# Head preparation and softmax rows in the projection's run of a two-block transformer kernel

## The chip, the cores and the metric

The kernel runs on one core of a Trainium2 chip. The metric is the device time of one execution in microseconds. A core has a matrix engine (TensorE, PE in the profile), VectorE (DVE), ScalarE (ACT) and GpSimd (POOL), and a queue engine, SyncE (SP), which here only issues DMAs. ScalarE issues a few DMAs too. Every engine runs its own list of instructions in order; semaphores order them against each other.

## What is computed

The reference is a pair of transformer blocks over 512 tokens of width 1024. The part that matters is the attention of the first block. One projection gives the inputs of three mixers (batch left out, 64 wide heads):

```
h = rms_norm(x, norm_mix);  proj = h @ w_in
a_q, a_kv, a_g, b_qkv, c_qkv = split(proj)
# a: 4 query heads on one key head, three branches: compressed, selected, window
#    q and k normed per head; compressed keys/values = gelu((kv + pe) @ w1) @ w2
# b: dilated heads, 3 groups of 2, q and k normed per head
#    s = q.k * scale - slope * distance;  p = softmax(s);  out = p @ v
# c: stick breaking, 6 heads:
#    z = q.k * scale;  a = exp(log_sigmoid(z) + sum_after(log_sigmoid(-z)))
cat = concat([o_a, o_b, o_c]);  x = x + cat @ w_out
```

Then come the squared-ReLU layer, and a second block with a recurrence, a convolution, two cross attentions and two gated feed-forward layers. None of that is touched.

## The kernel before

Matrices in full precision are split into a rounded high half and a rest, both of a rounded float32 type, and multiplied in three passes (hi·hi, hi·lo, lo·hi). That is `Linear`: for every output tile of 128 rows it does 24 matmuls of 512 columns. Weights come from SP in chunks of 512 KB, four slots deep; ScalarE makes the high half of a chunk two chunks ahead (`split_hi`), GpSimd the rest (`split_lo`). Small products that are not split run in plain float32.

`Projection` hangs on the `Linear` that makes the 24 projection tiles, in the order of `TILES`: stick tiles first, then queries, keys and values of the other mixers, three value tiles last. Functions are called once a tile on each engine: `in_tensor` after a tile's matmuls, `in_scalar` after ScalarE's split of the step, `in_vector` (which evicts the tile from its PSUM bank, t mod 4), and `in_pool`. From tile 6 on, three tiles carry one of the six stick heads: after part 0's tile TensorE does the values of the head before and this head's scores (`z`), ScalarE takes absolute values and exponentials, in part 1 ScalarE takes logarithms and VectorE the softplus, and after part 2's tile TensorE sums logarithms with a triangular matrix (`accumulate`), which waits for VectorE's remainders (`softplus_rest`, signal `softplus_lo`). Head 5 has tiles 21, 22 and 23, so its sums come after the last tile, and its values after that.

`run` gives one block of the program: all engines meet at its end. Three blocks follow each other: the projection, then `prepare_mixers`, then `softmax_mixers`. `prepare_mixers` loads the compression weights `cw` (2 MB), a table of picks, and the distance tables `dist`, all from SP. ScalarE squares ten tiles; TensorE sums the squares by head (L1119), turns four value tiles (L1110), does the compression (L1127), and spreads the inverse roots over a tile's rows (`L1140`, plain float32, four PSUM banks); VectorE takes the reciprocal (L1195) and multiplies (L1198). `softmax_mixers` takes four blocks of 128 queries, with 18 rows of scores each. It is staged one block ahead: scores of block qb + 1 stand among the transposes and values of block qb, and two packed tiles of the output projection (`partial`) stand before the first transpose. For a row TensorE writes scores (L1287), VectorE adds the distances and takes the minimum (`biased`, L1358), ScalarE takes exponentials (L1430), VectorE makes the weights of the 18 rows together (`weigh`), GpSimd and VectorE scale, and TensorE transposes (L1303).

## Time and profile before

| | |
|---|---|
| median of 3 runs | 2438.26 us (2438.21 to 2439.14) |
| the profiled execution's own time | 2442.83 us |
| its span, first to last instruction | 2441.1 us |
| TensorE busy | 2346.0 us (96%) |
| VectorE, ScalarE, GpSimd busy | 1124.9, 945.9, 1083.5 us |
| mean granted TensorE clock | 0.986 of full |
| end of the last projection tile | 203.6 us |
| first instruction of the preparation, of the softmax rows | 211.6, 240.7 us |

Busy shares are means over very different stages: what a change in one stage is worth is read from what TensorE waits for there, and for how long. The granted clock is 1.00 (2.4 GHz) or 0.50 (1.2 GHz); a value between them is a stretch that has both.

### The profile page before, as it was taken

What the parts mean: (1) busy time and instruction counts of PE and PEld (TensorE: products, weight loads), DVE (VectorE), ACT (ScalarE), POOL (GpSimd) and SP (SyncE); (2) the same over time, 40 slices, a digit from 0 to 9 for tenths busy, and PEclk for the clock granted to TensorE, in tenths of its full rate; (3) what the DMA queues carried; (4) which work ended last, traced back from release to release, by engine and by line L of the source; (5) the groups of instructions that cost most, each with busy time, mean ns of one, the idle gap of its engine ahead of it and who ended that gap; (6) DMA issues with size and microseconds to landing.
All of it is one profiled execution on the core that took longest, in us unless ns stands there. A gap on an engine that the chain in (4) does not pass through costs nothing.

```text
span 2441.1 us, 35228 instructions
## 1 busy us (share of the span) xinstructions
PE 2346.0 (96%) x13656; PEld 1866.7 (76%) x13656; DVE 1124.9 (46%) x1866; ACT 945.9 (39%) x1586; POOL 1083.5 (44%) x936
## 2 busy tenths in 40 slices
PE   7999999999989998989999999999999999999998
PEld 5776567888866777859878888888668777888887
DVE  5234544203125698535233660552697432651462
ACT  3565563212227563444333231233234534232222
POOL 4341455444541343337625445346235525445444
PEclk9999899999999999999999999999999999999999
DMA  3222002222421210024312223232113222223222
GB/s 130 70 69 92 18 27 95 95 95 95 154 84 35 69 61 10 3 84 133 104 44 87 95 95 112 78 104 97 60 60 122 78 69 77 89 93 114 78 101 69
DMA packets 57372, 198.10 MB, mean 81 GB/s; under 512 B 6544, under 2 KB 10768, under 8 KB 56592
## 3 DMA queue, kind: packets, MB, share of 16 engines
q1 hardware_dynamic: 54288, 191.70, 23.4%
q10 hardware_dynamic: 2944, 4.48, 0.5%
q8 instruction: 95, 1.56, 0.3%
q14 instruction: 45, 0.37, 0.1%
HBM read 194.05 MB, written 2.10 MB: 80 GB/s over the span
## 4 chain that ended last, share of the span: by engine, by line
PE 48%; DVE 6%; ACT 1%; issue 0%; POOL 0%; DVEq 0%; ACTq 0%
PE ps L370 11%; PE ps L372 11%; PE ps L371 11%; DVE ps L3005 4%; PE ps L445 3%; PE ps L447 3%; PE ps L446 3%; PE ps L2848 1%; PE ps L2871 1%; PE ps L3018 1%; DVE ps L3167 0%; PE ps L2608 0%; PE ps L2858 0%; PE ps L3062 0%; PE ps L2612 0%; DVE ps L2983 0%
## 5 line engine op out<-in xcount | busy, mean ns | idle before, releaser
L469 POOL TENSOR_TENSOR w_lo<-raw,w_hi 128x512 fp32r<-128x512 f32 x342 | 448.2, 1310 | 936.4 <-ACT w_hi L461 936.2
L370 PE MATMUL ps<-ahead_hi,w_hi 128*128 128x512 f32 x1216 | 481.3, 396 | 1.9 <-issue 1.9
L372 PE MATMUL ps<-ahead_hi,w_lo 128*128 128x512 f32 x1216 | 473.6, 389 | 0.0
L371 PE MATMUL ps<-ahead_lo,w_hi 128*128 128x512 f32 x1216 | 473.4, 389 | 0.0
L470 POOL TENSOR_TENSOR w_lo<-raw,w_hi 128x512 fp32r<-128x512 f32 x342 | 452.0, 1322 | 0.0
L461 ACT ACTIVATE w_hi<-raw 128x1024 fp32r<-128x1024 f32 x342 | 353.0, 1049 | 171.9 <-PE ps L447 91.0
L738 DVE TENSOR_TENSOR x_stream<-x_stream,ps 128x512 f32<-128x512 f32 x79 | 54.3, 688 | 469.9 <-PE ps L372 279.4
L370 PEld LDWEIGHTS ps<-ahead_hi,w_hi 128*128 128x128 f32 x1216 | 228.4, 188 | 52.7 <-issue 6.4
L371 PEld LDWEIGHTS ps<-ahead_lo,w_hi 128*128 128x128 f32 x1216 | 228.5, 188 | 50.7 <-issue 4.1
L372 PEld LDWEIGHTS ps<-ahead_hi,w_lo 128*128 128x128 f32 x1216 | 228.4, 188 | 47.8
L3139 ACT ACTIVATE ffn_s<-ps 128x512 f32<-128x512 f32 x44 | 26.3, 598 | 322.3 <-DVE ps L3167 322.3
L445 PE MATMUL ps<-ffn_a_hi,w_hi 128*128 128x512 f32 x342 | 133.6, 391 | 3.0 <-DVE ffn_a_lo L3172 2.9
L3005 DVE SCALAR_TENSOR_TENSOR ps<-conv_u,vecs,ps 128x512 f32<-128x512 f32 x192 | 127.1, 749 | 14.5 <-PE ps L3018 14.5
L446 PE MATMUL ps<-ffn_a_lo,w_hi 128*128 128x512 f32 x342 | 133.2, 389 | 0.0
L447 PE MATMUL ps<-ffn_a_hi,w_lo 128*128 128x512 f32 x342 | 133.2, 389 | 0.0
L775 POOL TENSOR_TENSOR squares<-squares,sqr 128x512 f32<-128x512 f32 x55 | 73.2, 1331 | 111.0 <-ACT sqr L764 65.6
L3150 DVE TENSOR_TENSOR ffn_u<-ps,root 128x512 f32<-128x512 f32 x88 | 60.6, 688 | 133.2 <-PE ps L372 133.1
L3167 DVE SCALAR_TENSOR_TENSOR ps<-ffn_u,vecs,ps 128x512 f32<-128x512 f32 x176 | 119.8, 749 | 0.0
L370 PE MATMUL ps<-hidden_hi,w_hi 128*128 128x512 f32 x256 | 99.7, 389 | 0.0
L371 PE MATMUL ps<-hidden_lo,w_hi 128*128 128x512 f32 x256 | 99.6, 389 | 0.0
L372 PE MATMUL ps<-hidden_hi,w_lo 128*128 128x512 f32 x256 | 99.6, 389 | 0.0
L370 PE MATMUL ps<-h_hi,w_hi 128*128 128x512 f32 x192 | 78.8, 410 | 16.3 <-DVE w_lo L251 13.8
(454 smaller groups left out, 4486.3 us busy)
## 6 DMA issues: line engine op xcount, KB each, us to landing
raw<-in_wall SPq DMA_DIRECT2D x346, 512.0 KB, 3.3
x_stream<-in_x SPq DMA_DIRECT2D x8, 256.0 KB, 7.6
cw<-in_cmp_w SPq DMA_DIRECT2D x1, 2048.0 KB, 7.8
out_y<-x_stream SPq DMA_DIRECT2D x16, 128.0 KB, 1.9
lora_a<-in_lora_a ACTq DMA_DIRECT2D x1, 1280.0 KB, 10.4
dist<-in_consts SPq DMA_DIRECT2D x1, 1088.0 KB, 10.9
lora_b<-in_lora_b ACTq DMA_DIRECT2D x1, 1024.0 KB, 5.1
mem<-in_mem SPq DMA_DIRECT2D x1, 1024.0 KB, 5.9
```

Source lines behind the costliest of these rows:

```text
L370: pe.matmul(out, hi, src.hi[:, t, 0:width], start=first, stop=False)
L371: pe.matmul(out, hi, src.lo[:, t, 0:width], start=False, stop=False)
L372: return pe.matmul(out, lo, src.hi[:, t, 0:width], start=False, stop=last)
L445: pe.matmul(out, hi, src.hi[:, q, 0:width], start=(q == 0), stop=False)
L446: pe.matmul(out, hi, src.lo[:, q, 0:width], start=False, stop=False)
L447: mm = pe.matmul(out, lo, src.hi[:, q, 0:width], start=False, stop=(q == kt - 1))
L461: e.activation(self.w.hi[:, s, :], self.raw[:, s, :], ACT.Copy).then_inc(hi_r.sem, 1)
L469: e.tensor_tensor(self.w.lo[:, s, 0:512], self.raw[:, s, 0:512], as_float(self.w.hi[:, s, 0:512]), ALU.subtract)
L470: e.tensor_tensor(self.w.lo[:, s, 512:1024], self.raw[:, s, 512:1024], as_float(self.w.hi[:, s, 512:1024]), ALU.subtract).then_inc(lo_r.se ...
L775: e.tensor_tensor(k.squares[:, :], k.squares[:, :], sqt[:, m % 2, :], ALU.add).then_inc(ac.sem, 1)
L3005: v.scalar_tensor_tensor(bank, self.u[:, m, t:t + T], self.tap(m, t), bank, ALU.mult, ALU.add).then_inc(self.added.sem, 1)
L3167: e.scalar_tensor_tensor(bank, ub[:, m % 4, t:t + T], col, bank, ALU.mult, ALU.add).then_inc(cv.sem, 1)
```

## The change

The two blocks after the projection become stages of the projection's run, `Heads` and `Softmax`; no border is left between the three. What moves:

- Squares go from ScalarE to VectorE, one tile behind the eviction, into tiles and value places that are free by then. The compression weights come in four pieces, with three small tensors, by seven DMAs that ScalarE issues in its step 7. The picks (10 x 128 columns) become 20 columns, which ScalarE expands.
- After tile 20 TensorE does the compression; after tile 21 the head sums and the small products; ScalarE takes GELU in step 20 and the roots in step 21; VectorE the reciprocal in step 21.
- The inverse roots are kept as a rounded value and a rest, in rows 32 apart, so that spreads run in the rounded type. Three spreads stand after tile 22, ahead of the last stick head's accumulation; the other seven stand among the matmuls of tile 23. VectorE multiplies after the last head's remainders.
- The distance tables lie where the projection's inputs were. SP loads them after tile 23's matmuls.
- The first 18 rows of scores have places of their own: 16 need no eviction, rows 16 and 17 wait for eight biased rows. After them come the last head's values and the four turns of value tiles, then two scores of the next block and the partial products.

The core of the diff:

```diff
+    def load(self, act):                      # Heads
+        self.done(act.dma_start(self.pos[:, :], a["cmp_pe"]), "cmp_small", 16)
+        self.done(act.dma_start(self.w2[:, :], a["cmp_w2"]), "cmp_small", 16)
+        self.done(act.dma_start(self.fan_raw[:, :], a["consts"][:, c:c + 2 * HEAD_TILES]), "cmp_small", 16)
+        for j, n, t in self.w1:               # four pieces
+            self.done(act.dma_start(t[:, :, :], a["cmp_w1"][:, j:j + n, :]), "cmp_loaded", 16)
...
         # Projection.in_tensor
-        if h >= 0 and part == 2:
+        if h >= 0 and part == 2 and h < self.H - 1:
             for u in range(4 * h, 4 * h + 4):
                 self.accumulate(pe, u)
+        if t == N_PROJ - 4:
+            self.heads.compress(pe)
+        elif t == N_PROJ - 3:
+            self.heads.summed(pe)
+        elif t == N_PROJ - 2:
+            self.heads.begin_spreads(pe)
+            for u in range(4 * h, 4 * h + 4):
+                self.accumulate(pe, u)
+
+    def amid(self, pe, t, q):
+        if t == N_PROJ - 1 and q:
+            self.heads.spread(pe, q + 2)
...
         # in_scalar
+        if t == self.FIRST + 1:
+            self.heads.load(act)
...
+        if t == N_PROJ - 4:
+            self.heads.gelu(act)
+        elif t == N_PROJ - 3:
+            self.heads.roots(act)
+        elif t == N_PROJ - 2:
+            self.heads.rounded(act)
...
         # in_vector, ahead of the eviction
+        if t >= 1:
+            self.heads.square(v, t - 1)
+        if t == N_PROJ - 2:
+            self.softplus(v, h)
+            self.heads.rests(v)
         v.wait_ge(self.used.sem, self.used(t + 1))
...
+        if t == 12:
+            self.heads.raws(v)
+        elif t == N_PROJ - 3:
+            self.heads.inverses(v)
+        elif t == N_PROJ - 2:
+            for n in range(HEAD_TILES):
+                self.heads.normed(v, n)
...
     def sync(self, sp):
-        pass
+        sp.wait_ge(self.used.sem, self.used(N_PROJ))
+        self.heads.distances(sp)
...
+    def spread(self, pe, t):
+        if t >= 3:
+            self.wait(pe, "heads_normed", t - 2)
+        self.done(pe.matmul(self.k.ps[:, t % 3, :], self.fan[:, t * P:(t + 1) * P],
+                            self.stacked[:, :], start=True, stop=True), "heads_spread")
+
+    def begin_spreads(self, pe):
+        self.wait(pe, "fan_made", 1)
+        self.wait(pe, "heads_rests", 2)
+        self.wait(pe, "cmp_rt", 1)
+        pe.wait_ge(self.pj.free.sem, self.pj.free(N_PROJ - 2 + 1 + RING))
+        for t in range(3):
+            self.spread(pe, t)
+        self.wait(pe, "cmp_done", 2)
...
         # Softmax, scores of a row
+            if qb:
+                pe.wait_ge(bi.sem, bi(U if g == U else g - 3))
+            elif u < 16:
+                self.heads.wait(pe, "heads_normed", 9 if u < 8 else 10)
+            else:
+                pe.wait_ge(bi.sem, bi(8))
+            if qb == 0 and u == 8:
+                pe.wait_ge(projected.sem, projected(N_PROJ + RING))
...
+        for u in range(U):
+            scores(0, u)
+        self.pj.values(pe, self.pj.H - 1)
+        for i in range(Heads.TURNS):
+            self.heads.turn(pe, i)
...
         # Softmax, ScalarE
+        for u in range(6):
+            exponentials(0, u)
+        self.pj.rounded(act, self.pj.H - 1)
+        for i in range(3):
+            self.heads.turned(act, i)
+        for u in range(6, U):
+            exponentials(0, u)
+        self.heads.turned(act, 3)
+        merged(0)
...
-                run(k, start, projection.linear(hs, start.handed), projection)
+                heads = Heads(k, a, projection, start, kc, vc, top)
+                softmax = Softmax(k, a, projection, heads, start)
+                run(k, start, linear, projection, softmax)
-            prepare_mixers(k, a, pr, vt, far, kc, vc)
-            softmax_mixers(k, pr, vt, gates, dist, dist_cmp, kc, vc, cat)
```

`roots` on ScalarE, in this order: the turn of the hidden values, a square, the expanded picks (`fan_made`), the root of the head sums, the root of the key sum. `rounded` rounds the inverses, `rests` (VectorE, two instructions of 32 rows) makes their remainders.

## Rows read from the trace of the kernel before

**Rows 1.** The page, busy time of TensorE.
```profile
PE 2346.0 (96%) x13656; PEld 1866.7 (76%) x13656; DVE 1124.9 (46%) x1866; ACT 945.9 (39%) x1586; POOL 1083.5 (44%) x936
```

**Rows 2.** Timeline of TensorE: start, duration, operation, count, [idle before].
```profile
187.73 2.37 PE L998 MATMUL ps<-sb_at,values 128*64 128x512 f32 x8
...
192.38 0.51 PE L370 MATMUL ps<-h_hi,w_hi 128*128 128x512 f32 x1
...
203.64 0.22 PE L985 MATMUL ps<-sb_parts_hi,negs 128*128 128x128 f32 x1
...
211.62 0.63 PE L1110 MATMUL ps<-consts,proj 128*128 128x128 f32 x4 [1.68 <-PEq L555]
...
218.33 3.67 PE L1119 MATMUL ps<-hn_sq,consts 128*64 128x512 f32 x12 [0.20 <-ACT hn_sq L1165]
221.92 7.18 PE L1127 MATMUL ps<-cw,craw 64*31 64x128 f32 x128
229.03 3.70 PE L1140 MATMUL ps<-hn_rt,dist 128*128 128x512 f32 x8
...
250.65 0.72 PE L1303 MATMUL ps<-consts,sm_pc 128*31 128x128 f32 x2 [1.16 <-POOL sm_pc L1480]
```

**Rows 3.** Timeline of ScalarE.
```profile
192.91 1.55 ACT L1014 ACTIVATE sb_sp<-sb_sp 128x256 f32<-128x256 f32 x4
...
195.43 1.28 ACT L1020 ACT_TABLE_LOAD   x1
196.72 1.93 ACT L1020 ACTIVATE sb_sp<-sb_sp,eps 128x128 f32<-128x128 f32 x4
198.55 1.05 ACT L461 ACTIVATE w_hi<-raw 128x1024 fp32r<-128x1024 f32 x1
199.55 2.02 ACT L1054 ACTIVATE sb_parts_hi<-sb_sp 128x128 fp32r<-128x128 f32 x4
...
222.18 0.78 ACT L1171 ACTIVATE hn_rt<-ps,consts 128x512 f32<-128x512 f32 x1
...
248.25 0.39 ACT L1430 ACTIVATE sm_p<-sm_p,sm_st 128x128 f32<-128x128 f32 x1
...
248.64 0.47 ACT L1437 ACTIVATE sm_st<-sm_st 128x3 f32<-128x3 f32 x2
```

**Rows 4.** Timeline of VectorE.
```profile
198.26 0.69 DVE L878 TENSOR_TENSOR proj<-ps,root 128x512 f32<-128x512 f32 x1 [6.82 <-PE ps L372]
...
200.46 3.99 DVE L1060 TENSOR_TENSOR sb_parts_lo<-sb_sp,sb_parts_hi 128x128 fp32r<-128x128 f32 x4
...
222.99 3.35 DVE L1195 RECIPROCAL hn_rt<-hn_rt 128x512 f32<-128x512 f32 x1 [7.66 <-ACT hn_rt L1171]
230.19 3.32 DVE L1198 SCALAR_TENSOR_TENSOR proj<-proj,vecs,ps 128x512 f32<-128x512 f32 x4 [3.85 <-PE ps L1140]
```

**Rows 5.** Timeline around stick head 0: VectorE's remainders, TensorE's last accumulation.
```profile
79.23 3.91 DVE L1060 TENSOR_TENSOR sb_parts_lo<-sb_sp,sb_parts_hi 128x128 fp32r<-128x128 f32 x4 [0.46 <-ACT sb_parts_hi L1054]
...
83.37 0.44 PE L985 MATMUL ps<-sb_parts_hi,negs 128*128 128x512 f32 x1
```

**Rows 6.** SP's queue, then one DMA issue: count, KB, us to landing.
```profile
203.97 0.33 SPq L352 DMA_DIRECT2D raw<-in_wall  x1
...
212.44 0.42 SPq L1099 DMA_DIRECT2D dist<-in_consts  x1
...
lora_b<-in_lora_b ACTq DMA_DIRECT2D x1, 1024.0 KB, 5.1
```

**Rows 7.** Windows (PEclk: granted clock), and TensorE's timeline at 1098.
```profile
249.00:254.00 5.00, 2.76 (x15) 1.16 (x15) 4.36 (x20) 1.06 (x6) 3.92 (x8) 1.00 0.00 2
255.00:274.00 19.00, 18.65 (x75) 10.15 (x75) 8.77 (x46) 11.97 (x51) 6.91 (x10) 0.50 0.00 0
1097.00:1104.00 7.00, 5.93 (x26) 5.90 (x27) 7.00 (x16) 5.02 (x10) 1.28 (x1) 0.54 0.23 75
...
1098.07 0.55 PE L370 MATMUL ps<-ms_hi,w_hi 128*128 128x256 f32 x1 [4.28 <-DVE ms_lo L2712]
```

More of the change, by code:

```diff
@@ L907, in tensor @@
     def tensor(self, pe):
-        self.values(pe, self.H - 1)
+        pass
     def scalar(self, act):
-        self.rounded(act, self.H - 1)
+        pass
     def vector(self, v):
-        self.rest(v, self.H - 1)
+        pass
     def turn(self, pe, i):
@@ new lines, in compress, with gelu, head_sum @@
+                        self.done(mm, "cmp_hidden")
+    def gelu(self, act):
+        for c in range(2):
+            self.wait(act, "cmp_hidden", c + 1)
+            self.done(act.activation(self.hid[0:N_CMP, c, :], self.k.ps[0:N_CMP, 2 + c, 0:128], ACT.Gelu_apprx_tanh), "cmp_gelu")
+    def head_sum(self, pe, t):
+        tile = self.TILES[t][0]
+        c, o, n = CST["own"] + 2 * HEAD_TILES - 2 - t // 2 * 2, 64 * (t % 2), self.order().index(tile)
+        self.wait(pe, "heads_squared", n + 1)
+        self.done(pe.matmul(self.k.ps[o:o + 64, 0, :], self.k.consts[:, c:c + 64], self.sq[n], start=(t < 2),
+                            stop=(t >= len(self.TILES) - 2)), "heads_summed")
@@ new lines, in rounded, with rests @@
+    def rounded(self, act):
+        self.wait(act, "heads_inverse", 1)
+        self.done(act.activation(self.stacked[:, :], self.rt[:, :], ACT.Copy), "heads_stacked")
+    def rests(self, v):
+        self.wait(v, "heads_stacked", 1)
+        for o in (32, 96):
+            at = self.stacked[o:o + 32, :]
+            self.done(v.tensor_tensor(at, self.rt[o:o + 32, :], as_float(at), ALU.subtract), "heads_rests")
+    def spread(self, pe, t):
[3 more added lines that the diff above has]
+                            self.stacked[:, :], start=True, stop=True), "heads_spread")
@@ new lines, in begin_spreads, with normed @@
+    def begin_spreads(self, pe):
[6 more added lines that the diff above has]
+        self.wait(pe, "cmp_done", 2)
+    def normed(self, v, t):
+        tile, gain = self.TILES[t]
+        self.wait(v, "heads_spread", t + 1)
+        self.done(v.scalar_tensor_tensor(self.pr[:, tile, :], self.pr[:, tile, :], self.k.vec("gains", gain),
+                                         self.k.ps[:, t % 3, :], ALU.mult, ALU.mult), "heads_normed")
@@ new lines, in distances, with turn @@
+    def distances(self, sp):
+        sp.dma_start(self.far[:, :], self.a["consts"][:, N_KEEP:CST["fan"]]).then_inc(self.k.sig("distances_loaded").sem, 16)
+    def turn(self, pe, i):
+        b0 = 5 + i % 3
+        if i == 0:
+            self.pj.wait(pe, "weights_raw", 4 * self.pj.H)
+            pe.wait_ge(self.pj.free.sem, self.pj.free(N_PROJ + RING))
+        if i >= 3:
+            self.wait(pe, "values_turned_out", i - 2)
+        for b in range(NB):
+            mm = pe.transpose(self.k.ps[:, b0, b * P:(b + 1) * P], self.pr[:, V_TILES[i], b * P:(b + 1) * P], self.k.ident)
+        self.done(mm, "values_turned")
@@ new lines, in scalar, with gpsimd @@
+                if u in (8, 14):
+                    rounded(qb, u // 6 - 1)
+                if u == 3 and qb < 3:
+                    part.split_hi(act, 0, qb)
+                if qb + 1 < NB:
+                    for t in range(3 * (u - 1) // 2, 3 * u // 2):
+                        if 0 <= t < U:
+                            exponentials(qb + 1, t)
+                    if u == 13:
+                        merged(qb + 1)
+            rounded(qb, 2)
+    def gpsimd(self, gp):
+        k, U, part, probs, stats, W = self.k, self.U, self.part, self.probs, self.stats, self.W
+        wt, scaled = k.sig("weights", "scaled_by_pool")
+        for qb in range(NB):
+            gp.wait_ge(wt.sem, wt(2 * (qb + 1)))
+            for u in range(U):
+                if u % 3 == 2:
+                    continue
+                t = probs(qb, u)
+                gp.tensor_scalar(t, t, stats(qb, W)[:, u:u + 1], None, ALU.mult).then_inc(scaled.sem, 1)
+            if qb < 3:
+                part.split_lo(gp, 0, qb)
@@ L3408, in constants @@
     u = np.arange(2 * HEAD_TILES - 2 + WIDE)[None] - (2 * HEAD_TILES - 2)
-    c["own"] = (p // 64 == u) | (p // 64 == u - 64)
+    c["own"] = (p // 64 == u) | (p // 64 == u - 32) | (p // 64 == u - 64)
     c["spread"] = (p % 64 == np.arange(D)[None] // 64)
-    c["fan"] = np.concatenate([(p == 64 * (m % 2) + 2 * (m // 2) + q // 64) for m in range(HEAD_TILES)], axis=1)
-    tile = p % 64 // 2 * 2 + p // 64
-    query = tile < HEAD_TILES // 2
-    head = np.where(tile < 2, 6 + 2 * tile, 2 * (tile - 2)) + p % 2
+    m, half = np.arange(2 * HEAD_TILES)[None] // 2, np.arange(2 * HEAD_TILES)[None] % 2
+    row = 64 * (m % 2) + 2 * (m // 2) + half
+    c["fan"] = (p == row) | (p == row + 32)
+    tile = p % 32 // 2 * 2 + p // 64
+    first = np.array([Heads.FIRST_HEAD[n] if n in Heads.FIRST_HEAD else -1 for n in range(32)])[tile]
+    query = first >= 0
+    head = np.where(query, first, 0) + p % 2
     squared = np.array(SLOPES)[np.where(query, head, 0)] ** 2
```

713 lines of the change are left out of this document (357 added, 356 removed).

## The prediction

> **What bounds the kernel now.** I read the page first: TensorE is busy for 96% of the span [rows 1], the other engines for less than half. So a stage is worth only what it leaves TensorE idle, or keeps it on work that another form would shorten. Then I read the timeline of each engine around the edit, from 187.7 us (last matmul of projection tile 21, which I call 0 below) to 250.65 us (first transpose of softmax weights) [rows 2]. That stretch lasts 63.0 us. From tile 23's end (203.64) to 250.65 it is 47.0 us. In it TensorE does the last head's sums (2.8), values (2.4), transposes and head sums (8.5), the compression (7.2), the spreads and small products (10.1), 18 scores, and 18 packed partial products (4.2). The rest is two block borders and waits for ScalarE. Everything before tile 21, and everything after the first transpose, keeps its instructions; only the clock and seven DMA issues reach there.
>
> **What TensorE's work becomes.** Moved at equal cost: compression 7.2, ten head sums at 0.61 each (3.67 for six), values 2.4, partial products 4.2. Ten spreads change from plain float32 at 0.92 each (3.70 for four) to the rounded type. The projection's rounded 512-column products start every 0.235 us (48 of them from 192.38 to 203.64 [rows 2]), so ten cost 2.3 and save 6.9. Two block borders fall away (1.68 for the first [rows 2], the second alike). Work alone would sum to 30.6 us where 47.0 stood, 16.4 less. The question is what waits come in.
>
> **Squares, and DMA issues on ScalarE.** Squares move to VectorE, behind each tile's eviction. VectorE idled 6.8 us ahead of an eviction [rows 4], so I cost them at nothing; if that cover were gone it would be about 1 us each. Loads of the compression weights and three small tensors leave SP, which has nothing else to do, and become seven issues on ScalarE in its step 7. An issue takes 0.42 us [rows 6], and with the gap to the next 0.46, so 3.2 us. Behind them in ScalarE's queue stand head 0's logarithms, and behind those softplus, rounding, VectorE's remainders and TensorE's accumulation. ScalarE ran that stretch without a pause, the remainders ended at 83.14, and the last accumulation that needs them started at 83.37 [rows 5]. There is 0.2 us of slack, so I add 3.0 us. The lower bound is 0, if issuing did not block the engine; the upper 3.5. The Trainium skill (DMA: Bandwidth & Descriptors, Issuing engines are not separate DMA queues) says that another issuing engine saves only issue time. Here that time is moved onto the busy engine; by that rule the transfers gain nothing, and the sum stays as it is.
>
> **Tile 21 to the start of tile 23.** Compression stands before tile 21: +7.2. Then, from 0: values and the last head's scores end at 4.65, as before. Six head sums, two small products, four sums and the key sum bring TensorE to 11.8, and tile 22 (5.6) to 17.4. Now ScalarE: its four exponentials ended at 6.7 before (192.91 + 1.55 [rows 3]). GELU has evicted the exponential table, so a load of 1.28 comes first and they end at 8.1. Then the turn of the hidden values and a square (9.4), the expanded fan, 1280 columns, which I take as 1.3 from a 1024-column copy of 1.05 [rows 3] (10.7), a table load (11.9), the root at 0.78 (12.7), a small root, a weight split (14.0), the load of the logarithm's table (15.3), four logarithms at 1.93 (17.2), the rounding of the inverses (17.8), a split (18.9), four roundings at 2.02 (20.9).
>
> VectorE takes the reciprocal from 12.7 to 16.1 (3.35 us [rows 4]), small steps to 16.8, four softplus adds (the 1.6 between the eviction and the remainders [rows 4], the last behind the last logarithm) to 18.5, and then the two remainders of the inverses. A 512-column remainder takes between 1.0 and 1.6 us by whether GpSimd splits weights beside it (four remainders of the stick parts, 1280 columns in all, took 3.99 [rows 4]). Two end at 20.6 to 21.7; I take 21.2, for a split of GpSimd begins at 18.9. Only then comes tile 22's eviction, 0.69 [rows 4]: 21.9. TensorE must have both before its first spread, so it stands idle from 17.4 to 22.0, 4.6 us. This is the price of the accumulation being ahead of tile 23, with the spreads: the chain that tile 23's 5.6 us of matmuls used to cover is bare. VectorE's stick remainders then end at 24.8, the last head's final accumulation at 26.2, and tile 23 begins there. With seven spreads in its middle it ends at 33.4. Ten gain multiplications at 0.83 each (3.32 for four) keep ahead of the spreads from the second on. Before, this point stood at 16.0 (203.7); now it is 33.4 after 7.2.
>
> **From tile 23's end, E, to the first transpose.** The distance table lies over the projection's input halves, so SP may load it only after E. Before it stands the last weight chunk, issued 0.3 us after tile 23's end in the old trace too [rows 6]. A 1024 KB load takes 5.1 us [rows 6] and 1.6 MB go together, so it lands at E + 6.3 to 7.0. I take 6.6. In the old order it was issued at 213.4 and lay hidden behind 24 us of preparation. Eight biased rows later (1.4 together, E + 8.0) TensorE may write scores 16 and 17, which share banks with the first eight; it has idled since E + 2.6, some 5.5 us, with values and transposes queued behind. Then values to E + 11.0, transposes to 12.8 (the fourth a little later), the partials to E + 17.5. ScalarE does six exponentials, the rounding of the last head, three evictions (to 13.4), twelve exponentials at 0.39 [rows 3] (18.1), the fourth eviction and the merge (19.1). Merge end to transpose was 1.54 [rows 2, 3], so the first transpose comes at E + 20.6, with ScalarE last. I take 20.4.
>
> **The sum at full clock.** 3.0 + 7.2 + 33.4 + 20.4 = 64.0, against 63.0: +1.0 us. Sixteen microseconds of removed work and borders are given back as two bare stalls (4.6 and 5.5), ScalarE's serial chain and the issues. I hold this sum to about 2.5 either way.
>
> **The clock.** The profile grants either all of 2.4 GHz or half. From 249 to 254 TensorE was busy for 2.76 of 5 us, and from 254.4 the clock was 0.50 until 274.9 [rows 7]. After an idle time of 4.28 us, ended at 1098.07, the dense rounded products that followed ran mostly at half: the clock read 0.54 from 1097 to 1104, with 5.93 us of work [rows 7]. So 6 us of work cost nearly 3 us more than at full. Both new stalls are at least as long. After the first, the low stretch falls on sums that wait for VectorE anyway and on tile 23: +2 (1 to 3). After the second it falls on values (2.4) and transposes (2.4), which would double, and part of the partials; ScalarE's evictions wait for them: +3 (1 to 4.5). What was cold after the first transpose would begin its cold time up to 4 us earlier, +0.7. That is +5.7, and with the sum +6.7.
>
> **The profile's own time** was 2442.83 us for a span of 2441.1, and the median of the runs shown is 2438.26, 4.6 below. The difference is taken as it is: 2438.3 + 6.7 = 2445.0 us.
>
> **Rivals.**
> First: the stalls come, but the clock holds or its cost falls where TensorE waits anyway. The sum is then +1.0 (-1.5 to +3.5), 2439.3. For it speaks that a clock fall is short after dense work, and that the accumulations have slack; against it, that each idle time over 3.5 us in the trace was followed by 0.5. Chance 0.30.
> Second, on the other side: the softmax stage no longer goes cold. Between 255 and 274 TensorE was 18.65 us busy at half clock [rows 7]; half of that, 9.3, is the most that full clock could give, and with ScalarE and GpSimd then setting part of the pace I take 6.5. The place is the pair of waits before and after the first transpose: if their idle time comes out under about 1 us instead of the old 2.1, it decides so. Time: +1.0 + 2.0 for the first stall - 6.5 = -3.5, and with the first stall also short -5.5 or more, 2433. Against it: ScalarE is last at E + 20.4 while TensorE is done at 17.5. Chance 0.08.
> Third: the change does what its removed work says and waits are nearly hidden, through a table landing early and a short chain at tile 22: 3.0 - 16.4 = -13.4, 2425. The rows contradict it at two places that the code fixes by waits. Chance 0.04.
> Fourth: both falls last as long as the softmax stage's did (20 us), +12 to +15: 2451 to 2453. Chance 0.08.
> The Trainium skill (ScalarE: Activation LUTs, What ACT_TABLE_LOAD costs) gives 2.66 us for a switch of tables, drain included. Here the load is 1.28 and the next activation starts 0.01 us after it [rows 3]. By that page three switches on the chain would lengthen the first stall by up to 4.2 us, and the total to 2449; the measured row is used.
>
> **Numbers.** Forecast 0.50, first rival 0.30, second 0.08, third 0.04, fourth 0.08. A difference of 0.2%, 4.9 us, is about what a measurement of this kernel can tell from none. Of the forecast's range (+3 to +10), two thirds lie above 4.9 us: slower 0.34 + 0.08 and 0.05 of the first rival, together 0.47. Same: 0.16 of the forecast, 0.25 of the first rival, and half of the second, 0.04, with a rounding 0.41 in all. Faster: the other half of the second, the third, and 0.04 for a stall that I have placed wrong, 0.12. The likeliest case alone reaches from 2441 to 2448; the range that leaves out no more than 2 in 10 is 2434 to 2451.
>
> **What would show each step.** In the new trace: no block border between tile 23 and the transposes; spreads at 0.23 us apart; a TensorE gap of about 3 us in all within head 0's accumulations near 83 us; an idle time of 4 to 5 us before the first spread, ended by VectorE; one of 5 to 6 us before scores 16 and 17, ended by VectorE, itself released by the table's DMA; granted clock 0.5 after each. The prediction is wrong if the issues do not hold ScalarE, if the table lands before E + 4, or if the clock after the stalls stays at 1.00.

## The result, and the profile after

The changed kernel takes 2444.82 us (median of 9 runs, 2443.49 to 2446.30), against 2438.26 us (9 runs, 2435.89 to 2439.15) for the kernel before. The ratio is 1.0025, 95% interval 1.0016 to 1.0034: slower by 0.25%, some 6 us. Forecast were 2445.0 us and "slower" as the likeliest of three. The profiled execution took 2443.49 us for a span of 2441.8. The sum comes out; its terms do not, and the experiments below are about that.

The page first. TensorE's busy time is 4.1 us below that of [rows 1], and the span did not follow. Even the 4.1 us hang on the execution that is compared with: a second one of the kernel before (experiment 1) has TensorE busy for 2341.7 us, as here.

```profile
span 2441.8 us, 35221 instructions
...
PE 2341.9 (96%) x13646; PEld 1865.4 (76%) x13646; DVE 1131.8 (46%) x1878; ACT 940.6 (39%) x1577; POOL 1087.8 (45%) x936
```

TensorE's timeline, from the end of tile 21's matmuls to the last partial product that stands in the softmax stage (columns as in [rows 2]):

```profile
197.08 2.37 PE L1035 MATMUL ps<-sb_at,values 128*64 128x512 f32 x8
...
217.29 1.58 PE L1290 MATMUL ps<-hn_hi,fan 128*128 128x512 f32 x3 [3.39 <-DVE proj L907]
...
222.50 0.44 PE L373 MATMUL ps<-h_hi,w_hi 128*128 128x512 f32 x1
...
229.84 0.45 PE L1419 MATMUL ps<-kc,proj 64*128 64x31 f32 x4
...
237.33 0.80 PE L1419 MATMUL ps<-proj 64*128 64x128 f32 x4 [4.72 <-DVE sm_st L1502]
238.06 3.92 PE L1035 MATMUL ps<-sb_at,values 128*64 128x512 f32 x8
241.91 2.03 PE L1320 MATMUL ps<-consts,proj 128*128 128x128 f32 x16
...
251.14 0.75 PE L1435 MATMUL ps<-consts,sm_pc 128*31 128x128 f32 x2 [2.53 <-POOL sm_pc L1636]
252.85 2.07 PE L1419 MATMUL ps<-proj 64*128 64x256 f32 x6 [0.96 <-DVE x_stream L1536]
...
367.73 0.39 PE L450 MATMUL ps<-cat_hi,w_lo 128*128 128x512 f32 x1
```

The lines show both stalls where the prediction has them, 3.39 us before the first spread and 4.72 before scores 16 and 17. There is no block border, and the first transpose starts at 251.14, where the kernel before had 250.65 [rows 2]. So up to there the change cost 0.5 us, by these two profiled executions.

What released the stalls stands in VectorE's timeline: the inverses' remainders and tile 22's eviction before the first spread, and the distance table's DMA before the first biased row.

```profile
209.55 3.35 DVE L1267 RECIPROCAL hn_rt<-hn_rt 128x512 f32<-128x512 f32 x1 [2.87 <-ACT hn_rt L1254]
...
215.02 1.40 DVE L1284 TENSOR_TENSOR hn_hi<-hn_rt,hn_hi 32x512 fp32r<-32x512 f32 x2
216.45 0.69 DVE L907 TENSOR_TENSOR proj<-ps,root 128x512 f32<-128x512 f32 x1
...
235.93 0.19 DVE L1502 CUSTOM_DVE_ANT_0 sm_pc<-dist,ps 128x31 f32<-128x31 f32 x1 [4.63 <-DMA dist<-in_consts]
```

SP's queue issued that DMA at 230.39, 0.55 us behind the last weight chunk, and it took 5.5 us to land:

```profile
229.84 0.33 SPq L355 DMA_DIRECT2D raw<-in_wall  x1
230.39 0.34 SPq L1309 DMA_DIRECT2D dist<-in_consts  x1
```

The windows give the granted clock (PEclk, the third value from the right) in each stretch:

```profile
217.00:221.00 4.00, 3.71 (x13) 3.29 (x14) 4.00 (x7) 1.74 (x3) 2.82 (x4) 0.57 0.02 4
234.00:241.00 7.00, 3.67 (x8) 1.48 (x9) 3.43 (x36) 2.26 (x12) 0.00 (x0) 0.53 0.17 71
241.00:251.00 10.00, 7.61 (x43) 5.79 (x41) 2.40 (x11) 7.47 (x31) 0.52 (x2) 0.99 0.01 2
251.00:279.00 28.00, 26.48 (x100) 15.38 (x101) 12.34 (x62) 14.03 (x60) 14.45 (x22) 0.51 0.01 2
279.00:367.00 88.00, 83.08 (x596) 57.41 (x595) 42.52 (x122) 54.04 (x155) 43.88 (x40) 1.00 0.10 30
```

The clock fell to its lower level (1.2 GHz, "half clock" below) behind each stall, as expected, for 3.4 and 6.8 us. But the long stretch is the third: from 251.5 to 278.8, 27.3 us, just where the softmax stage's small matmuls begin. I call the time from the first transpose to the last partial product (251.14 to 367.73, the same work in both kernels) the softmax stage from here on. It took 116.6 us; in the profile of before 250.65 to 364.94, 114.3 us.

### The profile page after: what moved, and what is told of

The parts are those of the page before. It is cut to its first block, busy times and chain, and to the rows that moved or that the text cites. A ratio compares the mean times of both kernels' runs of the same rounds, so it can differ in the third digit from the quotient of the medians.

```text
span 2441.8 us, 35221 instructions
## 1 busy us (share of the span) xinstructions
PE 2341.9 (96%) x13646; PEld 1865.4 (76%) x13646; DVE 1131.8 (46%) x1878; ACT 940.6 (39%) x1577; POOL 1087.8 (45%) x936
## 4 chain that ended last, share of the span: by engine, by line
PE 47%; DVE 7%; ACT 1%; issue 0%; POOL 0%; DVEq 0%; ACTq 0%
PE ps L373 11%; PE ps L375 11%; PE ps L374 11%; DVE ps L3160 5%; PE ps L448 3%; PE ps L449 3%; PE ps L450 3%; PE ps L3003 1%; PE ps L3026 1%; PE ps L3173 1%; DVE ps L3322 0%; PE ps L2763 0%; PE ps L3013 0%; PE ps L3217 0%; DVE ps L3138 0%; PE ps L2767 0%
## 5 line engine op out<-in xcount | busy, mean ns | idle before, releaser
L373 PE MATMUL ps<-h_hi,w_hi 128*128 128x512 f32 x192 | 79.4, 414 | 15.5 <-DVE w_lo L254 13.7
```

The source lines that it names most:

```text
L373: pe.matmul(out, hi, src.hi[:, t, 0:width], start=first, stop=False)
```

## The experiments

Every kernel was timed in several executions (11 for most, 8 in experiment 2, 12 in 6, 5 each in 11 and 12) beside the kernel before, and the ratios are to that one. Its own median was 2437.97 us beside experiments 1 to 4, 2438.63 beside 5, 6, 9 and 10, and 2437.64 beside 7, 8, 11 and 12, so a difference between two experiments is good to about 1 us. "Stage" is the softmax stage in the kernel's one profiled execution.

**1. The kernel before, profiled again.** No edit. It shows by how much one profiled execution of the same kernel differs from another.

> The kernel before, once more, with a profile of its own. The profiled execution of before was 4.6 us above the median of its timed runs, that of after was not above its own. Theory A (the difference of the medians, 6.6 us, arises in the projection's tail and in what the clock does there): a fresh trace has the first softmax transpose near 250.6 us or up to 1 us earlier, and its time is 2436 to 2440. Rival B (the difference comes from where half-clock stretches fall in later stages, and has little to do with the edit's waits): the fresh trace lacks one or more of the old trace's later half-clock stretches while its tail is the same. Ratio to before: 1.000 within 0.001 by both.

Measured: 2438.88 us, ratio 1.0004 (0.9995 to 1.0013). Its profiled execution took 2437.29 us, span 2435.6. TensorE's timeline, and three windows:

```profile
251.60 0.38 PE L1303 MATMUL ps<-consts,sm_pc 128*31 128x128 f32 x2
252.40 1.30 PE L1287 MATMUL ps<-proj 64*128 64x256 f32 x6 [0.42 <-DVE x_stream L1392]
...
361.48 0.39 PE L447 MATMUL ps<-cat_hi,w_lo 128*128 128x512 f32 x1
```

```profile
242.00:249.00 7.00, 7.00 (x38) 6.26 (x37) 3.63 (x32) 6.99 (x39) 0.00 (x0) 0.51 0.01 2
251.00:266.00 15.00, 12.72 (x80) 7.20 (x78) 8.53 (x47) 12.48 (x57) 7.93 (x13) 1.00 0.00 0
266.00:273.00 7.00, 7.00 (x27) 5.17 (x26) 3.35 (x17) 0.93 (x4) 6.39 (x10) 0.51 0.12 28
```

Here the stage starts at full clock and has 6.8 us of half clock, not 20.5 as in [rows 7], and it takes 109.9 us, 4.4 less. TensorE did not wait before the first transpose: a half-clock stretch of 6.8 us from 242.1 had drawn out the scores and partial products up to it. The idle time ahead of the scores, 1.65 us, was the same in both executions of this kernel, and only in this one did the clock fall behind it. Of the distance between the two executions (5.5 us of span) -1.0 lies ahead of the first transpose, 4.4 in the stage and 2.1 behind it.

Which of the two is the usual one? One profile can't say, but each timed execution has its mean granted clock over the whole kernel. Of the 86 executions of the kernel before that were timed beside the experiments, 61 have 0.987 or more, as this profile (0.988), and their median time is 2437.6 us. The other 25 have 0.986 or less, as the first profile (0.986), and a median of 2440.6. So the execution that [rows 1 to 7] come from belongs to the minority with more half clock. A mean over the kernel doesn't say where the clock was down.

This gives the accounting against a usual execution. After minus this: first transpose -0.5 us (251.14 against 251.60), stage +6.7 (116.6 against 109.9), all behind it 0.0 (2074.1 us in both). The sum, 6.2, is the difference of their times. Each of the two was the fastest of the executions timed with it, 1.3 and 1.6 us under their medians. The whole loss lies behind the first transpose, where the change edits nothing. Theory A had it in the stretch ahead of the transpose, and rival B in later stages; it is the stage between the two.

**2. The DMA issues one step earlier.** `self.heads.load(act)` at tile 6 instead of 7.

```
-        if t == self.FIRST + 1:
+        if t == self.FIRST:
             self.heads.load(act)
```

> Only the place of the seven DMA issues is changed, from ScalarE's step 7 to step 6, where ScalarE waited 4.9 us for the first scores. Theory A (issues stand in ScalarE's chain): head 0's sums are as early as in before, the trace gains 1.1 us or so against after at the first values (that is what the alignment of the two traces showed), total 2443 to 2444. Rival (the 1.1 us came from the transfers' traffic against the weights, not from issue time): no gain, 2444.8.

Measured: 2443.91 us, ratio 1.0026 (1.0015 to 1.0036); 0.9 us under the changed kernel, too little to tell. The trace tells more. In the changed kernel ScalarE's queue and TensorE's first sums of head 0 read:

```profile
73.32 0.34 ACTq L1164 DMA_DIRECT2D cpe<-in_cmp_pe  x1
...
76.43 0.45 ACTq L1169 DMA_DIRECT2D proj<-in_cmp_w  x1
76.92 1.28 ACT L1057 ACT_TABLE_LOAD   x1 [1.17 <-issue]
```

```profile
84.09 0.39 PE L1022 MATMUL ps<-sb_parts_hi,negs 128*128 128x256 f32 x1 [0.90 <-DVE sb_parts_lo L1097]
```

With the issues in step 6, the stick values of head 0 start at 90.42 us, as before (90.36); in the changed kernel at 92.41. Of those 2.05 us, 0.93 were there before the issues (a half-clock stretch at 22.8 us that the other two executions do not have), so the issues cost 1.1. The gain is still there at the end of tile 21 (195.06 against 197.08). They hold ScalarE for 1.17 us only, since its queue had begun to issue at 73.32 while the exponentials still ran. By the Trainium skill (DMA: Bandwidth & Descriptors, Issuing engines are not separate DMA queues) issuing on several engines saves only the time that it takes to issue. The queue that lost the issues here, SP's, had time to spare, and ScalarE paid for about a third of theirs, 1.17 us. No run here tests what the page says of the transfers themselves.

**3. A small early copy of the distance table.** The 128 columns that the first query block reads come by two more DMAs of ScalarE during tile 23, into a place that is free by then; the full table is waited for after the first block's rows.

```
+        elif t == N_PROJ - 1:
+            self.heads.load_near(act)
...
-        v.wait_ge(k.sig("distances_loaded").sem, k.sig("distances_loaded")(16))
+        v.wait_ge(self.heads.near_mark.sem, self.heads.near_mark(32))
```

> The part of the distance tables that the first 18 rows need (4 x 128 and 32 columns) is loaded a second time, by two issues of ScalarE at the end of its step 23, into projection tiles that are free by then; the full table comes as in after and is waited for only ahead of the second query block. Theory A (the table's landing sets the stall before scores 16 and 17, and that stall the clock's fall at 234.4): the 4.7 us idle time shrinks below 1, values and transposes run at full clock, the first transpose comes 5 to 8 us earlier, total 2437 to 2440. Rival (another wait stands right behind, ScalarE's exponentials or VectorE's evictions): below 2 us gained, 2443 to 2445.

Measured: 2438.86 us, ratio 1.0004 (0.9995 to 1.0013), 6.0 us under the changed kernel. TensorE's timeline:

```profile
231.76 1.66 PE L1430 MATMUL ps<-proj 64*128 64x128 f32 x20 [0.47 <-DVE proj L909]
233.35 2.37 PE L1037 MATMUL ps<-sb_at,values 128*64 128x512 f32 x8
...
244.86 0.63 PE L1446 MATMUL ps<-consts,sm_pc 128*31 128x128 f32 x2 [2.54 <-POOL sm_pc L1651]
```

The second stall is gone, the values take 2.37 us instead of 3.92, and the first transpose comes 6.3 us earlier, 5.8 counted from the end of tile 21. The stage is as slow as in the changed kernel: 116.9 us, 27.3 of them at half clock from 245.9.

**4. Both stalls filled with matmuls.** 13 rounded 512-column matmuls before the first spread, 18 before scores 16 and 17, into banks that are free.

```
+        for _ in range(13):
+            pe.matmul(self.k.ps[:, 3, :], self.fan[:, 0:P], self.pj.cat.hi[:, 3, :], start=True, stop=True)
...
+            if u == 16:
+                for _ in range(18):
+                    pe.matmul(k.ps[:, 5, :], self.heads.fan[:, 0:P], self.heads.stacked[:, :], start=True, stop=True)
```

> After's kernel with idle work for TensorE in its two stalls: 13 rounded 512-column matmuls whose result nobody reads ahead of the first spread, 18 ahead of score 16, 3.1 and 4.2 us at full clock, so that both fit into the idle times. Nothing else changes. Theory A (the clock falls because TensorE is idle there, and costs 2 to 5 us): granted clock 1.00 through the tail, total 2440 to 2443. Rival (the half-clock stretches cost nothing that shows, since ScalarE's chain sets the end): 2444 to 2446. If the filling itself delays what stands behind it, above 2446.

Measured: 2441.63 us, ratio 1.0013 (1.0004 to 1.0022), 3.2 us under the changed kernel. Its profiled execution was the slowest of its eleven (2446.64 us), so it doesn't explain the median. It shows the first fill doing its work and the second falling short:

```profile
216.42 0.94 PE L1290 MATMUL ps<-hn_hi,fan 128*128 128x512 f32 x3 [0.40 <-DVE proj L907]
...
238.13 0.80 PE L1425 MATMUL ps<-proj 64*128 64x128 f32 x4 [2.61 <-DVE sm_st L1512]
```

The spreads run at full clock. Tile 23 ends 1.5 us earlier (228.38 against 229.84), but 0.9 of that was there at the end of tile 21 (196.21 against 197.08), so this fill brought 0.6. The table took 7.8 us to land instead of 5.5, so 2.61 us stayed bare behind the second fill, and the clock fell again, for 6.8 us. The stage took 117.3 us. That the stalls' clock costs some 3 us together fits the median; the trace doesn't settle it.

**5. Matmuls around the first transposes.** 11 extra matmuls between the last partial product and the first transpose, and 4 behind the first two transposes, in the changed kernel:

```
+                self.heads.wait(pe, "values_turned_out", 2)
+                for _ in range(11):
+                    pe.matmul(k.ps[:, 6, :], self.cat.hi[:, 3, 0:P], self.cat.hi[:, 3, :], start=True, stop=True)
...
             turn(qb, 1)
+            if qb == 0:
+                for _ in range(4):
+                    pe.matmul(k.ps[:, 6, :], self.cat.hi[:, 3, 0:P], self.cat.hi[:, 3, :], start=True, stop=True)
```

> The changed kernel with 11 extra rounded 512-column matmuls on TensorE between the last packed partial product and the first transpose of softmax weights (idle 2.53 us there before), and 4 more between the first two transposes and the next scores (idle 0.96 us). They write a bank that is overwritten later, and nothing waits for them but TensorE itself. Theory A (the 27.3 us of half clock from 251.5 in the changed kernel follow from these idle times, and cost some 7 us against the 6.8 us of half clock in a usual execution of the kernel before): with the idle filled, first transpose to last partial product of the first softmax blocks takes 109 to 111 us instead of 116, and the total is 2438 to 2439, 6 to 7 us under the changed kernel. Theory B (the half clock there is set by the sparse matmuls of the softmax stage itself, whatever stands ahead of it): the stage still takes 116 us, and the total is 2444 to 2446.

Measured: 2439.89 us, ratio 1.0007 (0.9998 to 1.0016), 4.9 us under the changed kernel by adding 15 matmuls to it. TensorE's timeline, and the windows of the clock:

```profile
252.96 0.63 PE L1435 MATMUL ps<-consts,sm_pc 128*31 128x128 f32 x2
...
363.72 0.39 PE L450 MATMUL ps<-cat_hi,w_lo 128*128 128x512 f32 x1
```

```profile
252.00:268.00 16.00, 13.88 (x82) 7.79 (x83) 9.46 (x49) 12.45 (x56) 8.80 (x14) 1.00 0.00 0
268.00:275.00 7.00, 7.00 (x28) 4.96 (x29) 3.31 (x18) 1.18 (x6) 6.11 (x9) 0.51 0.07 17
```

Half clock fell from 27.3 to 6.8 us and the stage from 116.6 to 110.8. Theory A holds for the stage (109 to 111 us expected) and theory B falls; of the 6 to 7 us expected in the total, 4.9 came. The timed executions agree with the profile: their median granted clock is 0.986, that of the changed kernel 0.982.

**6. The same on top of the early copy**, that is the edits of experiments 3 and 5 together.

> The same extra matmuls on top of the kernel with the small early copy of the distance table, which measured 2438.9 and had 27.3 us of half clock from 245.9. Theory A: first transpose to last partial product 109 to 111 us instead of 116.5, total 2432 to 2433, below both kernels. Theory B: total 2438 to 2440, the stage 116 us.

Measured: 2433.59 us, ratio 0.9980 (0.9971 to 0.9989). The stage took 109.7 us (244.60 to 354.29), 3.4 of them at half clock. Against the early copy alone, 5.3 us less; 2432 to 2433 were expected.

**7. Only the matmuls ahead of the first transpose.** The second loop of experiment 5 is left out; the lines are against that experiment.

```
-                for _ in range(4):
-                    pe.matmul(k.ps[:, 6, :], self.cat.hi[:, 3, 0:P], self.cat.hi[:, 3, :], start=True, stop=True)
```

> The changed kernel with only the 11 extra matmuls ahead of the first transpose, and the idle time of some 0.8 us behind the first two transposes left open. If the idle time ahead of the first transpose alone starts the half clock, 2439 to 2441 as with both fills, and 109 to 111 us from the first transpose to the last partial product. If the second idle time is enough to start it, 2443 to 2445 and 115 to 117 us.

Measured: 2443.30 us, ratio 1.0021 (1.0012 to 1.0030). This is the second of the two cases expected: the wait ahead is not all that matters. TensorE and the window:

```profile
250.91 0.63 PE L1435 MATMUL ps<-consts,sm_pc 128*31 128x128 f32 x2
252.62 1.30 PE L1419 MATMUL ps<-proj 64*128 64x256 f32 x6 [1.08 <-DVE x_stream L1542]
```

```profile
254.70:275.20 20.50, 20.15 (x81) 11.34 (x82) 8.79 (x48) 12.57 (x55) 8.31 (x13) 0.50 0.00 1
```

Nothing stood idle ahead of the first transpose, 1.08 us behind it did. The clock fell 3.2 us later than in the changed kernel and stayed down for 20.5 us; the stage took 114.4. So 11 dense matmuls right ahead of the transposes don't keep the clock up by themselves, with the second idle time open. The reverse, only the second one filled, was not run.

**8. The same filling in the kernel before**, with 5 and 4 matmuls.

```
                 partial(qb, 1)
+                if qb == 0:
+                    for _ in range(5):
+                        pe.matmul(k.ps[:, 6, :], cat.hi[:, 3, 0:P], cat.hi[:, 3, :], start=True, stop=True)
                 turn(qb, 0)
                 turn(qb, 1)
```

> The kernel before with 5 and 4 extra matmuls at the same two places. In its profiled execution of 2442.83 us the softmax stage had 20.5 us of half clock, in its other profiled execution (2437.29) 6.8 us. If idle time ahead of the first transpose (1.16 us there) starts the long half clock in those executions that have it, the spread at the upper end shrinks and the median moves by -1 to +1 us. Rival: the kernel before is usually as slow in this stage as the changed one, so that filling takes off 4 us or more (2433 to 2435); then the growth of the half clock in the changed kernel would not be what cost 5 us.

Measured: 2439.07 us, ratio 1.0008 (0.9999 to 1.0017), runs from 2435.81 to 2444.48. The profiled execution has 6.8 us of half clock and a stage of 110.1 us, as experiment 1 without filling. That fits experiment 1: the kernel before usually has no long half clock to fill. That its upper end came from such stretches is not borne out: the spread did not shrink.

**9. The last head's accumulation behind tile 23**, where it stands in the kernel before. Three spreads go into the end of tile 23, the others between and behind the four accumulations.

```
-        if h >= 0 and part == 2 and h < self.H - 1:
+        if h >= 0 and part == 2:
             for u in range(4 * h, 4 * h + 4):
                 self.accumulate(pe, u)
+                if h == self.H - 1:
+                    self.heads.spread(pe, u - 4 * h + 3)
...
-        if t == N_PROJ - 1 and q:
-            self.heads.spread(pe, q + 2)
+        if t == N_PROJ - 1 and q >= 5:
+            if q == 5:
+                self.heads.begin_spreads(pe)
+            self.heads.spread(pe, q - 5)
```

> The changed kernel with the last stick head's accumulation where the kernel before has it, behind tile 23; the first three spreads go into the end of tile 23, the others between and behind the four accumulations. The prediction's term (a bare stall of 4.6 us ahead of the first spread, which tile 23's matmuls used to cover, with 2 us of clock behind it): no idle time over 1 us ahead of tile 23, tile 23 ends some 8 us earlier than in the changed kernel, the table is fetched as much earlier, the stall ahead of scores 16 and 17 is 3 us or less, since accumulations and spreads lie under the fetch; the first transpose comes 8 to 9 us earlier. Total then 2436 to 2438 if the softmax stage stays as slow as in the changed kernel, 2430 to 2432 if it runs as in a usual execution of the kernel before. Rival (the stall ahead of the spreads only moves, since ScalarE's chain sets the spreads and the end of the accumulation alike): the first transpose moves by under 3 us, total 2442 to 2445.

Measured: 2435.24 us, ratio 0.9983 (0.9974 to 0.9992), 9.6 us under the changed kernel. TensorE's timeline:

```profile
219.73 0.50 PE L1295 MATMUL ps<-hn_hi,fan 128*128 128x512 f32 x1 [0.62 <-DVE proj L1307]
...
225.62 0.48 PE L1421 MATMUL ps<-kc,proj 64*128 64x31 f32 x4 [0.81 <-DVE proj L1307]
...
226.97 2.50 PE L1421 MATMUL ps<-proj 64*128 64x128 f32 x20 [0.20 <-DVE proj L912]
...
241.33 0.63 PE L1437 MATMUL ps<-consts,sm_pc 128*31 128x128 f32 x2 [2.54 <-POOL sm_pc L1638]
```

Both stalls are gone: the longest wait left before the partial products is 0.81 us. Tile 23's matmuls cover the reciprocal's chain, and sums and spreads cover the table's fetch. The first transpose comes 9.8 us earlier. Of these, 1.2 were there at the end of tile 21 (195.85 against 197.08, the half clock at 22.8 us again), so the late accumulation brought 8.6, where 8 to 9 were expected. The stage stays slow, 115.8 us with 23.9 of half clock. The total is 0.8 us below the 2436 to 2438 expected for that case.

**10. That, the early copy, and the issues in step 6.**

> The late accumulation together with the small early copy of the distance table, and with the seven DMA issues in ScalarE's step 6 instead of 7. If stall one (ahead of the spreads) and stall two (ahead of scores 16 and 17) are separate costs, their removal adds up: the late accumulation alone leaves at most 3 us of stall two, so this lies 2 to 4 us below it, 2433 to 2435, or 2427 to 2429 if the softmax stage is no longer slow. If ScalarE's chain sets the first transpose once both stalls are gone, it lies within 1.5 us of the late accumulation alone.

Measured: 2433.97 us, ratio 0.9979 (0.9970 to 0.9988), first transpose at 239.51. It is 1.3 us under experiment 9. The total lies in the first range expected, but the distance is that of the last case (within 1.5 us). Once accumulation and spreads lie under the fetch, the early copy has little left to save: the wait before the last four scores is 0.23 us here. Whether ScalarE's chain then sets the first transpose, as that case says, was not tested.

**11 and 12. Both with the extra matmuls.** First experiment 10, then experiment 9, each with the 11 and 4 matmuls of experiment 5.

> All edits that helped, together: the late accumulation, the small early copy of the distance table, the DMA issues one step earlier, and the 11 and 4 extra matmuls around the first softmax transposes. The kernel without the extra matmuls measured 2433.97 and took 115.7 us from the first transpose to the last partial product, at half clock for 23.9 of them. If the half clock follows from the idle time of 2.54 us ahead of the first transpose, this takes 109 to 111 us there and 2427 to 2429 in all, 10 us below the kernel before. If after the shorter chain the clock falls anyway, it stays at 2433 to 2434.

> The late accumulation with the extra matmuls, without the early copy of the table and with the issues where the change has them. The late accumulation alone measured 2435.24, with 23.9 us of half clock. Expected 2429 to 2430 if the half clock follows from the idle time, and 1 to 2 us above the version that has the early copy too; 2434 to 2436 if not.

Measured: 2427.30 us, ratio 0.9955 (0.9941 to 0.9969), and 2427.05 us, with the same ratio and interval. For the second 2429 to 2430 were expected, 1 to 2 us above the first; it is no slower than the first. These beat both kernels: the one before by 10 to 11 us, the changed one by 17 to 18. The simpler of the two (late accumulation, extra matmuls) is the one to keep. Its TensorE:

```profile
237.58 2.65 PE L1476 MATMUL ps<-cat_hi 128*128 128x512 f32 x11
240.29 0.63 PE L1437 MATMUL ps<-consts,sm_pc 128*31 128x128 f32 x2
240.67 1.18 PE L1482 MATMUL ps<-cat_hi 128*128 128x512 f32 x4
...
351.01 0.39 PE L450 MATMUL ps<-cat_hi,w_lo 128*128 128x512 f32 x1
```

The stage took 110.7 us. Against experiment 9 the profiled spans differ by 8.5 us: 1.0 before the first transpose, 5.1 in the stage, and 2.4 behind it, where no instruction differs. So not all of the 8.2 us between the medians need be the filling's.

All profiled executions together, ordered by the idle time of TensorE ahead of the first transpose and behind the first two. The last column is the median granted clock of each kernel's timed executions, over the whole kernel:

| kernel | idle ahead, behind | half clock in the stage | stage | clock |
|---|---|---|---|---|
| 8, before, filled | 0, 0 | 6.8 us | 110.1 us | 0.988 |
| 11, late, early copy, filled | 0, 0.14 | 3.4 | 109.4 | 0.989 |
| 5, changed, filled | 0, 0.15 | 6.8 | 110.8 | 0.986 |
| 12, late, filled | 0, 0.15 | 6.8 | 110.7 | 0.989 |
| 6, early copy, filled | 0, 0.16 | 3.4 | 109.7 | 0.988 |
| 1, before again | 0, 0.42 | 6.8 | 109.9 | 0.987 |
| 7, filled ahead only | 0, 1.08 | 20.5 | 114.4 | 0.983 |
| before [rows 2] | 1.16, 0.96 | 20.5 | 114.3 | 0.988 |
| changed | 2.53, 0.96 | 27.3 | 116.6 | 0.982 |
| 4, stalls filled | 2.51, 1.08 | 27.3 | 117.3 | 0.985 |
| 2, issues in step 6 | 2.54, 1.08 | 27.3 | 117.2 | 0.9825 |
| 3, early copy | 2.54, 1.08 | 27.3 | 116.9 | 0.984 |
| 9, late accumulation | 2.54, 1.08 | 23.9 | 115.8 | 0.985 |
| 10, late, early copy | 2.54, 1.08 | 23.9 | 115.7 | 0.984 |

The stage's time follows its half clock without an exception: 109.4 to 110.8 us with 3.4 or 6.8 of it, 114.3 to 117.3 with 20.5 to 27.3.

## Why the prediction was right in the sum, and where its terms were not

**The work and its order: right.** No border, spreads 0.23 us apart behind tile 23's products, and the removed work given back as waits.

**Issues on ScalarE: mis-sized.** +3.0 forecast, 1.1 measured (experiment 2). The lower bound of 0 "if issuing did not block the engine" was nearer, and the "gap of about 3 us in all" near 83 us was not there.

**Tile 21 to E: place and order right, 2.6 us too long.** 33.4 forecast at full clock, and 2 for the clock, 35.4 in all; measured 32.8 with the clock in it (197.08 to 229.84). The stall was 3.39 us and not 4.6, mainly since the two remainders took 1.40 us together and not the 2.7 taken from 1280 columns of other shapes; the place and the releaser (VectorE, tile 22's eviction) were as written. The Trainium skill's 2.66 us for a table switch (ScalarE: Activation LUTs, What ACT_TABLE_LOAD costs) is not what this chain pays. ScalarE's rows on it are

```profile
207.44 1.28 ACT L1254 ACT_TABLE_LOAD   x1
208.74 0.78 ACT L1254 ACTIVATE hn_rt<-ps,consts 128x512 f32<-128x512 f32 x1
```

again 1.28 us, with the next activation 0.02 us behind it, and the activation before it ended at 207.42. The measured row was the right one to use; the page's figure would have made the stall longer still.

**E to the first transpose: the mechanism right, the time 2.1 us too long.** 20.4 at full clock and 3 for the clock; measured 21.3 (229.84 to 251.14). The table landed 5.5 us after its issue, at E + 6.1 (6.6 forecast), and the stall was 4.72 us (5.5). Values at half clock took 3.92 us (+1.5); the transposes I had doubled ran at full clock, 2.03 us. Experiment 3 prices the whole stall, clock included: 5.8 us of the timeline, 6.0 of the median.

**The clock behind the first transpose: the step that failed.** The prediction has "What was cold after the first transpose would begin its cold time up to 4 us earlier, +0.7", and took the 4.6 us between the profiled execution and the median "as it is". The long cold stretch of [rows 7] is not the usual case: experiment 1 has 6.8 us of half clock in the stage, and by their mean clocks so have most timed executions. Against it the changed kernel's 27.3 us cost +6.7, not +0.7. This made good what the other terms had too much: up to the first transpose 69.0 us were forecast (64.0 and 5 of clock) where 63.4 came, 5.6 less. So the total of 2445.0 is right by two errors of about the same size and opposite sign. That is luck. What the experiments show in its place: the idle time of 2.53 us ahead of the first transpose and 0.96 behind it bring on the long half clock, and filling them gives 4.9 us back (5), 5.3 (6) and 6.7 or 8.2 (11, 12). Of the two, the one behind was enough for 20.5 us (7).

**The rivals.** The first (clock costs nothing, 2439.3) falls. Its +1.0 up to the first transpose is near the +0.5 measured, but by chance, for the measured one has half clock in it. Its ground against itself, "each idle time over 3.5 us in the trace was followed by 0.5", leaves out the 13.80 us at the kernel's start, behind which the clock stayed at 1.00. The second had the right place, "the pair of waits before and after the first transpose", and the right mechanism, in the wrong direction: together the waits grew from 2.1 to 3.5 us. Experiment 5 is its case, with -4.9 us where it took -6.5. The third is contradicted by both stalls; experiment 12 comes near its 2425 with both removed and the clock mostly held. The fourth had a long fall right and its place wrong. In the chances, "same" adds up to 0.45 (0.16, 0.25 and 0.04), not 0.41: the 0.04 went to "faster" and is no rounding. The order of the three is the same either way.

**What stays open.** Why the half clock lasts 20 to 27 us in this stage when TensorE has waited at its start, and 3.4 to 13.7 elsewhere; why the clock falls behind an idle time in one execution and not in another of the same kernel; how much each of the two stalls costs in clock alone (experiment 4); and what starts the stretch behind the stage that goes with 2 us, below.

## What to carry to other kernels

Before a profiled execution is used as the base of a sum, ask where its distance to the median lies; here 4.4 of 5.5 us lay in the one stage that the change then touched without editing it. The mean clock of each timed execution tells which profile is the usual one. When a chain is shortened, look at the first sparse stretch behind it: a wait of 1 to 2.5 us at the border from dense matmuls to small ones cost 5 to 7 us there, and fifteen matmuls that compute nothing took it back. Moving work ahead of a tile uncovers the chain that the tile was hiding: the accumulation alone, put back behind tile 23, was worth 9.6 us of the median.

## What the runs showed of the hardware that was not expected

- Once down at the start of the softmax stage, the clock stayed at 0.50 for 20.5 to 27.3 us while TensorE was 26.48 of 28 us busy by the records (changed kernel). With the idle time ahead of it gone and at most 0.42 us behind, the clock was down for 3.4 or 6.8 us in the whole stage. Each extra microsecond at half clock cost 0.33 us of time (6.7 for 20.5, changed kernel against experiment 1).
- An idle time of 1.08 us, between sparse matmuls, was followed by 20.5 us at half clock (experiment 7); one of 0.42 us at the same place was not (experiment 1).
- The length of an idle time alone doesn't decide. In two executions of the kernel before the same wait of 2.37 us ends at 957.25 and 952.94. Behind it the clock fell in the first and stayed up in the second:

```profile
957.25 0.33 PE L2331 MATMUL ps<-S,W 64*64 64x64 f32 x4 [2.37 <-DVE S L2357]
957.00:961.00 4.00, 3.75 (x22) 3.27 (x23) 2.55 (x7) 1.78 (x4) 1.27 (x1) 0.57 0.00 0
...
952.94 0.33 PE L2331 MATMUL ps<-S,W 64*64 64x64 f32 x4 [2.37 <-DVE S L2357]
952.70:956.70 4.00, 3.76 (x67) 3.32 (x68) 2.73 (x8) 2.71 (x5) 1.28 (x1) 1.00 0.02 6
```

- Behind the stage, with the same instructions, the rest of the kernel took from 2073.5 us (experiment 8) to 2076.8 us (experiment 6). The six profiled executions that have a half-clock stretch of 3.4 us at that place, between 942 and 958 us (before, and experiments 6, 7, 9, 10 and 11) took 2076.0 us or more, the eight without it 2074.8 or less. 3.4 us at half clock can cost 1.7 by themselves; what starts the stretch, and whether it costs the rest, was not tested.
- A DMA queue can issue while the engine's earlier activations still run: the first of the seven issues started at 73.32 us, when the first of the four exponentials that stand before it had run for 0.08 us (it starts at 73.24).
